# The triangular inverse of the gated delta heads on 32 columns per tile, with its side work moved behind the steps of the scan and one ScalarE table set for logarithm and exponential

## What is computed

```python
g = jnp.cumsum(log_a, axis=-1)
decay = jnp.exp(jnp.where(causal, g[..., :, None] - g[..., None, :], -jnp.inf))
kk = jnp.einsum('bhncd,bhnsd->bhncs', k, k)
lmat = jnp.where(strict, beta[..., :, None] * decay * kk, 0.0)
rhs = jnp.concatenate([beta[..., None] * v, (beta * jnp.exp(g))[..., None] * k], axis=-1)
sol = lax.linalg.triangular_solve(jnp.eye(GDN_CHUNK, dtype=f32) + lmat, rhs,
                                  left_side=True, lower=True, unit_diagonal=True)
...
def step(s, inp):
    u0_c, w_c, aqk_c, qg_c, kg_c, gl_c = inp
    u = u0_c - w_c @ s
    o = qg_c @ s + aqk_c @ u
    s = gl_c[..., None, None] * s + jnp.swapaxes(kg_c, -1, -2) @ u
    return s, o
```

## Time and profile before

| | |
|---|---|
| time, median of 3 runs | 3962.32 us (3960.25 to 3966.88) |
| the profiled execution | 3973.05 us, of which its span is 3971.2 us |
| PE busy in the span | 3850.5 us (97%) |
| DVE busy | 2230.0 us (56%) |
| ACT busy | 826.7 us (21%) |
| POOL busy | 719.1 us (18%) |
| delta heads 0 to 3 | 486.35 to 737.66 us of the span |

### The profile page before, as it was taken

The page is one execution under the profiler, slowest core; times in us unless marked ns, Lnnn a source line. Parts: engine busy times, 40 slices in busy tenths (PEclk is TensorE's granted clock), DMA queues, the critical chain, the costliest instruction groups (busy, mean ns, idle before and its releaser), DMA issues.

```text
span 3971.2 us, 48569 instructions
## 1 busy us (share of the span) xinstructions
PE 3850.5 (97%) x18602; PEld 2881.5 (73%) x18602; DVE 2230.0 (56%) x3856; ACT 826.7 (21%) x1466; POOL 719.1 (18%) x570
## 2 busy tenths in 40 slices
PE   7999988999999999999999999999999999999998
PEld 3455567665555555678888877888789898778886
DVE  4255676354445322325556665664788888556546
ACT  2244455221010014632110101000311111110002
POOL 0048843100000000000000002120144343121200
PEclk9999989999999999999999999999999999999999
DMA  5244300131211121113322222232222222122321
GB/s 191 91 164 149 138 2 1 65 93 55 62 54 58 59 74 32 43 44 84 85 85 88 83 84 85 85 101 95 77 70 69 63 72 71 52 86 85 101 85 64
DMA packets 381407, 312.13 MB, mean 79 GB/s; under 512 B 9552, under 2 KB 349904, under 8 KB 381136
## 3 DMA queue, kind: packets, MB, share of 16 engines
q1 hardware_dynamic: 381264, 310.16, 25.0%
HBM read 308.03 MB, written 2.10 MB: 78 GB/s over the span
## 4 chain that ended last, share of the span: by engine, by line
PE 86%; POOL 5%; DVE 4%; ACT 3%; issue 1%; DMA 1%; POOLq 0%; SPq 0%; DVEq 0%; ACTq 0%
PE ps_lin L967 18%; PE ps_lin L867 10%; PE ps_d L967 9%; PE ps_lin L1742 6%; PE ps_d L867 5%; PE ps_c L967 4%; PE ps_lin L750 4%; PE ps_lin L767 3%; PE ps_lin L813 3%; PE ps_d L750 3%; PE ps_lin L1158 3%; PE ps_c L867 3%; POOL arena L3506 2%; PE ps_d L1531 2%; POOL arena L3503 2%; PE ps_c L750 2%
## 5 line engine op out<-in xcount | busy, mean ns | idle before, releaser
L3475 POOL TENSOR_TENSOR rstd<-square 128x512 f32<-128x512 f32 (+2 forms) x12 | 15.1, 1259 | 1555.3 <-ACT square L1920 1555.3
L967 PE MATMUL ps_lin<-arena,ring 128*128 128x256 f32 (+1 forms) x800 | 217.2, 424 | 1.1 <-DVE arena L2597 1.1
L867 PE MATMUL ps_lin<-arena,ring 128*128 128x256 f32 (+1 forms) x864 | 214.1, 401 | 0.0
L967 PEld LDWEIGHTS ps_lin<-arena,ring 128*128 128x128 f32 x800 | 151.8, 190 | 60.9 <-issue 2.9
L867 PEld LDWEIGHTS ps_lin<-arena,ring 128*128 128x128 f32 x864 | 164.2, 190 | 41.1
L967 PE MATMUL ps_lin<-hid_in,arena 128*128 128x256 f32 x832 | 188.6, 380 | 3.6 <-DVE arena L2624 3.6
L3478 POOL TENSOR_TENSOR rstd<-rstd,square 128x512 f32<-128x512 f32 (+2 forms) x58 | 76.0, 1310 | 630.5 <-ACT square L1920 629.5
L967 PE MATMUL ps_lin<-hid_in,mixed 128*128 128x384 f32 (+1 forms) x672 | 187.7, 432 | 0.0
L967 PE MATMUL ps_d<-arena,mixed 128*128 128x384 f32 (+1 forms) x672 | 187.7, 432 | 0.0
L2621 DVE TENSOR_TENSOR arena<-ring 128x1024 f32<-128x1024 f32 x84 | 103.0, 1226 | 146.3 <-PE ps_d L867 135.4
L967 PEld LDWEIGHTS ps_lin<-hid_in,arena 128*128 128x128 f32 x832 | 157.7, 190 | 27.7 <-DVE arena L2624 5.6
(11 more groups left out here) (555 smaller groups left out, 8234.1 us busy)
## 6 DMA issues: line engine op xcount, KB each, us to landing
ring<-in_ffn_w_in SPq DMA_DIRECT2D x88, 512.0 KB, 4.7
resid<-in_ada_w SPq DMA_DIRECT2D x20, 2048.0 KB, 7.9
ring<-in_mlp_w_up SPq DMA_DIRECT2D x64, 512.0 KB, 4.3
ring<-in_mlp_w_down SPq DMA_DIRECT2D x64, 512.0 KB, 4.4
ring<-in_attn_w_qkv SPq DMA_DIRECT2D x64, 512.0 KB, 4.8
ring<-in_ffn_w_out SPq DMA_DIRECT2D x32, 512.0 KB, 4.3
ring<-in_even_w_in SPq DMA_DIRECT2D x28, 512.0 KB, 4.9
ring<-in_sc_w_in SPq DMA_DIRECT2D x24, 512.0 KB, 4.8
```

Of the source, the lines that this page charges most:

```text
L867: last = mm(prod[i - 1], lhs[:, j, :], rhs(p), start=(g == j == 0), stop=(g == G - 1 and j == np_ - 1))
L967: last = mm(out, lhs[:, j, :], rhs[:, j, :], start=(j == 0), stop=(j == 3))
```

## The change

Three things are changed together.

**Levels on 32 columns.** Levels 1 to 4 build only the inverse of the four 32 x 32 diagonal blocks of a tile. They work on compact arrays `cX`, `cY`, `cS` (12 tiles x 32 columns in a new buffer `inverse`), in two halves d (the direction, six tiles each) instead of three groups of four tiles. Each product is on one of four 32 x 32 quadrants. Level 0 comes from products too (`turned_blocks`, with a 32 x 32 identity), not from a predicated copy of `gL`. Level 5 is `pair_products` and `pair_updates`, 32 x 32 blocks off the diagonal; ScalarE then copies the blocks into `gY` (`diagonal`, `pair`), VectorE into `gX`. Level 6 is as before.

**Side work one operation per step.** Most of the preparation of head n leaves the levels. The logarithms go between the two copies of w, and the rest goes behind single steps of the scan.

**One table set.** `logs()` loads by name a set that holds both the logarithm and the exponential.

```diff
+PAIR = LAST - 1
+R_CY, R_YCY, R_X, R_Y = 2 * (PAIR - 1) + 1 + 2, 2 * PAIR + 1 + 2, 2 * PAIR + 4 + 2, 2 * PAIR
-QUARTERS = (slice(0, 64), slice(64, 128))
+QUARTERS = tuple(slice(32 * q, 32 * q + 32) for q in range(4))
...
+    m["cX"], m["cY"], m["cS"] = (cut(inv, i * 384, 12, 32) for i in range(3))
...
# TensorE
+                def products(e, d):
+                    c = 2 * (e - 1) + d
+                    pe.wait_ge(s.r_y, R_Y * h + c + 1)
+                    if e == 1:
+                        pe.wait_ge(s.r_vt_out, h + 1)
+                    for t in range(NT):
+                        j = d * NT + t
+                        for r in QUARTERS:
+                            last = mm(CYB[d][r, t * 32:(t + 1) * 32], gL[r, j, r], cY[r, j, :], start=True, stop=True)
+                    last.then_inc(s.r_cy, 1)
...
+                for e in range(1, PAIR):
+                    for d in range(2):
+                        products(e, d)
...
+                    for d in range(2):
+                        updates(e, d)
...
+                pair_products()
+                pair_updates()
+                if n is not None:
+                    pe.wait_ge(s.r_kq_out, 2 * h + 2)
...
+                    delta_sums(n, 0, SIDE)
+                    delta_sums(n, 1, whole(psc))
...
+                if n is not None:
+                    pe.wait_ge(s.r_ln, 2 * n + 2)
...
+                    if i == 0:
+                        delta_decay(n, 0, SIDE)
+                    if i == 3:
+                        pe.wait_ge(s.r_qe, 2 * n + 1)
+                        delta_decay(n, 1, SIDE)
# ScalarE
-                act.preload_act_table(ACT.Ln)
+                act.preload_act_table_set("natural_log_exp_and_others")
...
+                gate_of(h)
+                if n is not None:
+                    logs()
                 for d in range(2):
                     act.wait_ge(s.r_w, 2 * h + d + 1)
                     fn(half(m["nwT"], d), tiles(psl[:, d, 0:T]), ACT.Copy).then_inc(s.r_w_out, 1)
-                if n is not None:
-                    exp_decay(n, 1)
+                    if n is not None:
+                        log_of(n, d, (SIDE, whole(psc))[d])
                 for i in range(NT):
...
+                    if i < 2:
+                        rstd_of_row(n, i)
+                    if i == 1:
+                        exp_gate(n)
+                    if i == 2:
+                        exp_rows(n, 0, SIDE)
+                    if i == 3:
+                        exp_decay(n, 0)
+                    if i == 4:
+                        exp_rows(n, 1, SIDE)
+                    if i == 5:
+                        exp_decay(n, 1)
# VectorE
+                for e in range(PAIR):
+                    for d in range(2):
...
+                        dve.copy_predicated(half(cY, d), over_tiles(m["levels"][:, e, d, :]), blocks(YCYB[d]))\
+                            .then_inc(s.r_y, 1)
+                        dve.wait_ge(s.r_y, R_Y * h + 2 * e + d + 1)
+                        dve.transpose(half(cX, d), half(cY, d)).then_inc(s.r_x, 1)
...
+                    if i == 1:
+                        differences(n, 0, SIDE)
+                    if i in (2, 3):
+                        normalise(n, i - 2)
+                    if i == 4:
+                        differences(n, 1, SIDE)
+                    if i == 5:
+                        beta_gate(n)
```

More of the change, by code:

```diff
@@ L82, in shape_constants @@
     lev = []
-    for b in range(LAST):
+    for b in range(PAIR):
         w = 1 << b
[L85 to L88, removed]
+        i, j = (p % 32)[:, None], np.arange(32)[None]
+        low = (i // (2 * w) == j // (2 * w)) & (i // w % 2 == 1) & (j // w % 2 == 0)
+        up = (i // (2 * w) == j // (2 * w)) & (i // w % 2 == 0) & (j // w % 2 == 1)
+        lev.append(np.stack([up, low], 1))
+    c["levels"] = np.stack(lev, 1).reshape(P, PAIR * 2 * 32)
     invp = np.zeros((P, 1), np.float32)
@@ L1373, in delta_head @@
                     delta_out_sums(h - 1, SIDE)
[L1374 to L1382, removed]
@@ new lines, in pair_updates @@
+                def pair_updates():
+                    pe.wait_ge(s.r_cy_out, R_CY * (h + 1) - 2)
+                    pe.wait_ge(s.r_x, R_X * h + 2 * PAIR)
+                    for t in range(NT):
+                        for d in range(2):
+                            j = d * NT + t
+                            for lo, up in PAIRS[d]:
+                                last = mm(YCYB[0][up, t * 32:(t + 1) * 32], cX[up, j, :], cS[up, t, :],
+                                          start=True, stop=True)
@@ new lines, in delta_head @@
+                for d in range(2):
+                    turned_blocks(d)
+                for t in range(NT):
+                    last = pe.transpose(psc[:, t * P:(t + 1) * P], gk[:, t * P:(t + 1) * P], ident)
+                last.then_inc(s.r_kt, 1)
+                for e in range(1, PAIR):
+                    for d in range(2):
+                        products(e, d)
+                    if e == 1:
+                        if h:
+                            pe.wait_ge(s.r_oln, h)
+                        for t in range(NT):
+                            c = slice(t * P, (t + 1) * P)
+                            last = mm(psd[:, c], gk[:, c], gq[:, c], start=True, stop=True)
+                        last.then_inc(s.r_kq, 1)
+                    for d in range(2):
+                        updates(e, d)
+                    if e == 2 and h == 0:
+                        mod_slot(H_EVEN - 1, MOD_STEPS)
@@ new lines, in delta_head, with diagonal @@
+                for e in range(1, PAIR):
+                    for d in range(2):
+                        act.wait_ge(s.r_cy, R_CY * h + 2 * (e - 1) + d + 1)
+                        fn(half(cS, d), blocks(CYB[d]), ACT.Copy).then_inc(s.r_cy_out, 1)
+                    if e == 1 and h:
+                        out_rstd(h - 1)
+                    if n is not None and e > 1:
+                        silu(n, e - 2)
+                def diagonal(q):
+                    fn(gY[q, :, q], cY[q, :, :], ACT.Copy).then_inc(s.r_parts, 1)
@@ new lines, in delta_head @@
+                dve.wait_ge(s.r_x, R_X * h + 2 * PAIR)
+                for d in range(2):
+                    for g in QUARTER[d]:
+                        dve.tensor_copy(half(gX, d)[g, :, g], half(cX, d)[g, :, :]).then_inc(s.r_x, 1)
+                dve.wait_ge(s.r_ycy, R_YCY * (h + 1) - 2)
+                for d in range(2):
+                    a, b = QUARTER[d]
+                    dve.transpose(half(gX, d)[b, :, a], blocks(YCYB[0][a, :])).then_inc(s.r_x, 1)
+                for d in range(2):
+                    causal(d)
```

330 lines of the change are left out of this document (139 added, 191 removed).

## The result

The changed kernel takes 3970.64 us (median of 17 runs, 3967.53 to 3974.37), against 3963.65 us for the kernel before, run beside it (17 runs, 3960.25 to 3973.6). The forecast was 3920, the range 3900 to 3945. It was wrong by 50.7 us.

The account below looks back on a forecast made before the run. TensorE, busy 97% of the span, was taken to bound the kernel, with VectorE and the engine chain pacing levels with side work. Savings of 34 us (delta heads) and 8.5 (table set), 42.5, gave 3920 us; range 3900 to 3945.

Parts of the forecast that it names:

- The levels: Delta heads, start to end of level 4: 9 ns a product, 2.2 us a level, 19.2 us in all.
- Rival (b): In the levels a small product costs what a larger one does, 29 ns: 64 us more, 3984, slower; chance 0.07.
- From there to the scan: Delta heads, after level 4: ScalarE works without a pause, TensorE waits for the second logarithm; 13.4 us.
- The scan: Scan of a middle delta head: 14.0 us as it is, with the moved side work 20.6.
- rival (a): Half clock, 1.2 GHz, in the scans of two more heads: 25 us more, 3945; chance 0.10.
- The stage's sum: Four delta heads: 205.6 us against 251.3, 45.7 less; after deductions of 8 and 4, 34 less.
- The clock: Delta heads: 20 us of full-speed TensorE time missing, 10 on the path, 8 of it left in the new stage.
- The table set: Outside the delta heads: 64 of 107 table loads go, most in TensorE's shadow; 8.5 us saved.
- From the profile to the median: Whole kernel: the saving of 42.5 us taken from the profiled 3973.05 (3930.5) and from the median 3962.3 (3920).

Follow-up runs that it names:

- half_left_out: The changed kernel with every second block of 32 rows left out in turned_blocks, products and updates, half the inverse's blocks not computed: 3932.63 us.
- rows_later: The changed kernel with ScalarE's exp_rows of the next head's second half moved from behind step 4 to behind step 5 of the scan: 3961.05 us.
- filled: The changed kernel with one extra 128 x 128 product on 512 columns behind each half of levels 2 to 4, and 1: 3970.24 us.
- set_only: The kernel before with the one table set for logarithm and exponential, nothing else: 3949.16 us, ratio 0.9961.

## Why the prediction was wrong, step by step

**The levels: the step that failed.** "I take 9" ns a product was right (48 in 0.62 us). What failed is the use of it: "A level is the chain product 0.64, copy 0.33, update 0.64, predicated copy 0.40 and four hand-overs of 0.05: 2.2 us", with "neither TensorE (1.7) nor VectorE (1.5) fills it" for the two halves. A third resource fills the level, TensorE's instruction supply. A level issues 2 x 192 instructions, 1.5 packets, at 3.7 us each 5.5 us; the forecast has 2.2. Head 1's start and levels took 27.29 us (552.30 to 579.59) against 19.2 forecast, and in half_left_out, where supply doesn't bind, 18.00 (546.60 to 564.60). The supply is worth up to 38.0 us of the 50.7 (3970.64 - 3932.63): half_left_out takes some work of the array out of the chain too. The pauses alone are 29.8. Rival (b) named the outcome (a small product costs as much as a larger one, decides from 23 ns on) with the wrong mechanism: 3.7 us / 128 is 29 ns, so in the long run it was true, and it had 0.07. The trace of before has the queue (97 packets of 16.4 kB, 1.59 MB; the closest two of its delta stage are 4.37 us apart), so one packet per 256 instructions could be read from it. What a faster pace would meet it doesn't show: it has no pause of this kind. The prediction put the term at nothing without having looked at that queue.

The Trainium skill has the supply: "Runtime: NRT & Kernel Launch", section "Instruction fetch mechanics", states refills in 16 KiB blocks of 256 instructions, and that fetch is hidden since instructions are dispatched more slowly than it fills. The first half agrees with the 16.4 kB and the 128 products; the second does not hold here, where 128 products and their loads run in 1.27 us and TensorE then waits 1.3 to 2.2.

**From there to the scan.** Forecast 13.4, measured 16.67 us in head 1 (579.59 to 596.26). ScalarE's gapless row up to the second logarithm, the load of 1.28 and TensorE's wait for it (3.32) came as described. Mis-sized: the two column sums, 2.7, took 2.93 + 1.53, the first at a granted clock of 0.50, and ScalarE waits 3.65 us for the corner products that stand behind them; and I left out the four `diagonal` copies of ScalarE (0.5 each) and the four copies of the blocks into `gX`, which took VectorE 3.56 us together while GpSimd worked (a cause that I didn't test).

**The scan.** Forecast 20.6, measured 24.25 (596.26 to 620.51). The hole ahead of the last step is 3.00 us by the trace, 3.1 in the forecast, from the copy of u behind `exp_rows`; rows_later removed it. The steps of 2.49 held. Mis-sized: the first step and the decay behind it, 5.6 us (596.26 to 601.82) where 1.5 and 1.3 stood. TensorE ran them at the half level (granted 0.50 there, 0.99 in the rest of the scan): products of 128 x 128 last 0.63 for two there and 0.39 in the next step. That is a piece of rival (a), and by its sign, 0.5 in a scan, it was there.

**The stage's sum.** With all that, half_left_out's stage is 224.61 us against 217.3 forecast (62.65, 58.24, 58.11 and 45.61 by head). So without the supply limit, and with half of the blocks' products, the stage is 7 us off. Some of that is in the sums: the parts named for the start and levels come to 20.2 us with the 1 us for phases that don't mesh, not 19.2, which is 4 us in four heads; and head 0 comes to 56.9 by its own terms (53.2 + 5.0 - 1.28), not 57.7.

**The clock.** "I leave 8 of it in the new stage, TensorE being no busier there": heads at 0.82, 0.78, 0.79 and 0.78 against 0.86, 0.95, 0.90 and 1.00. The clock fell further than I allowed. What that costs in time is not settled (filled); half_left_out, at 0.81 to 0.85, is fast all the same.

**The table set.** Forecast 8.5 outside the stage, measured 14.6 by the two traces. The norm ahead of 831 us and mix1 gave 1.3 each, as said (1.18 and 1.28), the end 1.1 (1.28; VectorE's last wait is 3.36, forecast 3.4). Not foreseen: 2.6 ahead of the delta heads (they start at 483.74, not 486.35), 2.6 in place of 1.28 around 1813 us, of which 1.3 come in the products behind the wait (the granted clock from 1800 to 1845 us was 0.96 before and is 1.00 now); and 6.3 instead of 3.5 in the second mixer's heads, where the waits of L1561 are gone as forecast, but most of them gave 0.7 us and not the 0.5 that the list has on average; 0.6 is lost later. set_only has the same time outside the stage, 3704.8 us, so this part is the table set's alone.

**From the profile to the median.** I made the sum on an execution of 3973.05 and carried the whole saving to a median of 3962.3. But the new heads had been built from full-speed rows, while the old ones, at clocks of 0.86 to 0.95, were slow ones: outside the stage the kernel before has 3719.9 us, and its median of 3963.65, whose span is about 3961.8, then leaves about 242 for the stage, not 251.3, if the rest takes the same in every execution. set_only, whose profiled execution is its median, bears that out: the same four heads in 242.61 us, at clocks of 0.95, 0.90, 0.97 and 1.00. So 251.3 was an unlucky draw of the profiled execution, and against 242 the levels and scans of the new kernel are 20 us slower, not 11.5. On the profiled execution the forecast was 3930.5, and the miss 39.5; the other 11 us are this step. (The table set saves nothing inside the stage by these two traces.)

The account, in us from 3920: supply +38.0, stage otherwise +7.3, luck of the profiled execution, counted as a saving, +11, table set -6.1: 3970. Of the first two only the sum, 45.5 = 262.84 - 217.3, is measured in the changed kernel; half_left_out divides it.

## What to carry to other kernels

Count instructions as a resource of its own. In these runs TensorE was not fed more than 256 instructions, 128 products with their loads, per 3.4 to 3.9 us over a longer stretch. Splitting products for the array's sake pays only while that rate is not reached. The sign of it is not "issue" alone, as the kernel before shows, but "issue" every 128 products, 1.2 to 1.6 us behind a packet of the instruction queue. Where idle time of that kind is there, work with few instructions hides in it, so spreading side work out of such a phase, as this change did, gives away its cover: moving some back gave 5 to 7 us. And when a saving is built from full-speed rows, compare it with the median's stage, not with that of the one profiled execution.

## What the runs showed of the hardware

- A refill reaches TensorE as a packet of 16.4 kB; in a long burst it ran 141 products, then 128, 128 and 115, with 1.31 to 2.18 us of nothing between. In the delta stages of all thirteen traces no two packets started closer than 3.29 us.
- Products by their size, issued without a wait: 32 x 32 in four places 9 to 14 ns, 64 x 64 in two places 29 ns, 128 x 128 on 32 columns 207 ns at a granted clock of 0.52, about 0.11 us at 1.00. That is what one on 128 columns costs (12 in 1.60 us, L1464), so a full-size product gains nothing from having few columns. The weight loads (PEld) are busy throughout that stretch too; that they set the price is likely, not tested.
- A long run of such products of 128 x 128 on 32 columns (106 us, TensorE busy throughout) was granted 0.52 of the full clock; 14 products on 512 columns more in head 1 (filled) raised its mean granted clock from 0.78 to 0.94.
- The table set alone is worth 14 to 18 us of 3965, with 64 loads of 1.28 us taken away: one fifth of their sum.
